# Sums of weight blocks for the second down stage: made by accumulating DMA instead of additions on Pool

## The chip, the cores and the metric

The kernel runs on one core of one Trainium2 chip. The metric is device time in microseconds (us) of one execution; lower is better. TensorE (PE) multiplies, VectorE (DVE), ScalarE (ACT) and Pool (GpSimd) work on tiles in SBUF, SyncE (SP) issues most loads. "HBM" and "DRAM" mean the same memory. DMA transfers of all queues run on the core's 16 DMA engines.

## The reference

One decoder layer on 512 tokens of width 1024: a SwiGLU feed-forward stage, a token-mixing stage of several attention branches, and a second feed-forward stage. What matters here is the frame and the feed-forward:

```python
def swiglu(x, w_gu, w_down):
    g, u = jnp.split(x @ w_gu, 2, axis=-1)
    return (jax.nn.silu(g) * u) @ w_down
...
        x = x + 0.5 * rms_norm(swiglu(rms_norm(x, ffn1_norm_pre[l]), ffn1_w_gu[l], ffn1_w_down[l]),
                               ffn1_norm_post[l])
        h = rms_norm(x, mix_norm_pre[l])
...
        x = x + rms_norm(merged @ w_out[l], mix_norm_post[l])
        x = x + 0.5 * rms_norm(swiglu(rms_norm(x, ffn2_norm_pre[l]), ffn2_w_gu[l], ffn2_w_down[l]),
                               ffn2_norm_post[l])
```

The inner width is D_FF = 2816, that is 22 blocks of 128 rows; all is float32. Each product is made of three products of rounded high and low parts.

## The kernel before

The stages follow one another: up products of the first feed-forward (to about 240 us), its down products (to 360 us, `down`, L2152), projections and attention (to 811 us), up products of the second feed-forward (to 1046 us), and its down products (`down_product`, L2178, and `down_rest`, L2197). Weights go through a ring of two slots: SP loads `ring_raw` (1 MB a slot in two DMAs), ACT copies it rounded into `ring_hi` (`hi`, L872), DVE subtracts into `ring_lo` (`lo`, L1327; in halves, L1338, before the projections), PE multiplies.

In the second down stage 16 of the 22 row blocks of the weight `w2_down` are not multiplied plainly but by a scheme of seven products in place of eight. For each of two groups g of 8 row blocks, the weight is cut into four blocks B11, B12, B21, B22 (4 x 128 rows by 512 columns each, 1 MB). Besides B11, B21 and B22 the scheme needs four sums T1 to T4 of blocks, and on DVE sums of the matching blocks of the activations (`sum_h`, from L1503), and on the finished products `close_21`, `close_22`, `close_12`. In the kernel before

T3 = B22 - B12, T1 = B12 - B11, T2 = T3 + B11 = B22 - B12 + B11, T4 = B21 - T2.

These eight sums (four for each g) don't depend on any input but the weight. Pool makes them ahead, in the first down stage, when the upper part of the activation memory is free, and stores them in DRAM as `down_weight_sums` (`sums_dram`). SP loads them into the ring in the second down stage (`load_down_block`, L607).

The order of Pool's program is written out by hand. After the first up stage (`rows_read(0)`) it loads a gain, issues the loads of the four blocks of g = 0 (`load_blocks(0)`, four buffers `down_block`, L744), builds a vector of position biases by 107 small copies (L773), stores it (L776), waits, and issues five DMAs that spread it over rows in DRAM (L784). Then come `sum_blocks(0)`, a wait for its four stores, `load_blocks(1)` into the same buffers, and `sum_blocks(1)`. Each `sum_blocks` is four additions (L751, L754, L757, L760), each followed by a store. After that stands `add_x(0)` (L729 to L735), and only then the wait for the last stores.

`add_x(0)` adds the normed result of the first feed-forward stage to x: six additions (L734) of 128x512, each after DVE has made `y_gained` (`add_y`, L1380). `y_gained` has room for two of the four token tiles, so DVE's work on tile 2 waits for Pool's first two additions, and on tile 3 for the first four. PE's `renew_x` waits for the first four additions before it transposes the new x (L2036), and the projection (L2012) waits for the transposed and scaled x. DVE reaches `add_y` only after it has split the first projection weights (L1338).

Of the kernel before, what the change touches and what calls it, by code (L numbers as in the profile page):

```python
# [29 lines left out]
ALU = mybir.AluOpType  # L30
# [3 lines left out]
P = 128  # L34
S, D, F = 512, 1024, 2816
# [146 lines left out]
def layer_kernel(nc, x, g1_pre, w1_gu, w1_down, g1_post, gm_pre, w_in, pos_k, cw1_k, cw2_k,  # L182
# [218 lines left out]
    blocks_loaded, sum_made, sums_stored = sem("blocks_loaded"), sem("sum_made"), sem("sums_stored")  # L401
# [175 lines left out]
    with block:  # L577
# [128 lines left out]
        def _(pool):  # L706
# [33 lines left out]
            def load_blocks(g):  # L740

                for block_sb, (k_half, c) in zip(blocks_sb, ((0, 0), (0, 1), (1, 1), (1, 0))):
                    k0 = 8 * g + 4 * k_half
                    pool.dma_start(block_sb[:, :, :], by_k(w2_down[k0 * P:(k0 + 4) * P, c * S:c * S + S])).then_inc(blocks_loaded, 16)  # L744

            def sum_blocks(g):

                b11, b12, b22, b21 = [b[:, :, :] for b in blocks_sb]
                t3, t1, t2, t4 = [sums_dram[g, i] for i in range(4)]
                pool.wait_ge(blocks_loaded, 64 * (g + 1))  # L750
                pool.tensor_tensor(b22, b22, b12, ALU.subtract).then_inc(sum_made, 1)  # L751
                pool.wait_ge(sum_made, 4 * g + 1)
                pool.dma_start(t3, b22).then_inc(sums_stored, 16)
                pool.tensor_tensor(b12, b12, b11, ALU.subtract).then_inc(sum_made, 1)  # L754
                pool.wait_ge(sum_made, 4 * g + 2)
                pool.dma_start(t1, b12).then_inc(sums_stored, 16)
                pool.tensor_tensor(b11, b22, b11, ALU.add).then_inc(sum_made, 1)  # L757
                pool.wait_ge(sum_made, 4 * g + 3)
                pool.dma_start(t2, b11).then_inc(sums_stored, 16)
                pool.tensor_tensor(b21, b21, b11, ALU.subtract).then_inc(sum_made, 1)  # L760
                pool.wait_ge(sum_made, 4 * g + 4)
                pool.dma_start(t4, b21).then_inc(sums_stored, 16)
# [3 lines left out]
            load_blocks(0)  # L766
# [8 lines left out]
            pool.wait_ge(vec_filled, 2)  # L775
            pool.dma_start(vec_dram, bias_vec[0:20, :]).then_inc(scratch_stored, 16)  # L776
# [8 lines left out]
            sum_blocks(0)  # L785
            pool.wait_ge(sums_stored, 64)
            load_blocks(1)
            pool.wait_ge(scratch_stored, 96)
            sum_blocks(1)

            add_x(0)
            pool.wait_ge(sums_stored, 128)
# [517 lines left out]
        def _(dve):  # L1310
# [85 lines left out]
            def ffn(base, f, p):  # L1396
# [107 lines left out]
                def sum_h(which, g):  # L1504
# [3 lines left out]
                    if which == 1:  # L1508
                        dve.wait_ge(w_used, first_down)
                        e = dve.tensor_tensor(h_sum[1, g][:, :, :], a21, a22, ALU.add)  # L1510
                    else:
                        dve.wait_ge(h_summed, H_SUMS.index((2 if which == 4 else 1, g)) + 1)
                    if which == 2:
                        e = dve.tensor_tensor(h_sum[2, g][:, :, :], h_sum[1, g][:, :, :], a11, ALU.subtract)
                    if which == 3:
                        e = dve.tensor_tensor(a21, a11, a21, ALU.subtract)
                    if which == 4:
                        e = dve.tensor_tensor(h_sum[4, g][:, :, :], a12, h_sum[2, g][:, :, :], ALU.subtract)
# [11 lines left out]
                def close_22(row):  # L1530

                    bank = ps[:, 5 + 2 * row, :]
                    dve.wait_ge(down_taken, 6 + row + 1)
                    dve.wait_ge(down_closed, 2 * row + 2)
                    dve.tensor_tensor(bank, bank, u3_sb[:, row, :], ALU.add).then_inc(down_closed, 1)

                def close_12(row):
# [4 lines left out]
                    dve.tensor_tensor(bank, bank, m5_sb[:, row, :], ALU.add).then_inc(down_closed, 1)  # L1542
# [1090 lines left out]
```

## Time and profile before

| what | us |
|---|---|
| median of 3 runs (1158.41 to 1161.01) | 1160.94 |
| profiled execution | 1163.08 |
| its span | 1161.4 |
| PE busy in the span | 1140.4 |
| DVE busy | 769.9 |
| ACT busy | 538.7 |
| Pool busy | 144.5 |
| share of the chain that ended last: PE | 91% |

The span runs from the first to the last instruction; the profiled execution's own time is 1.7 us longer. Busy time of an engine says how much it works, not what it holds up: that is read from waits (who was idle until whom) and from the chain that ended last. In the views below a row of a timeline is start, duration, engine, line, operation and tiles, and in brackets the idle time before it with its releaser.

### The profile page before, as it was taken

How to read it: one execution, taken by the hardware profiler on the slowest of the kernel's cores; microseconds unless marked ns; L12 is line 12 of the kernel's file. 1: busy time of each engine (PE TensorE's matmuls, PEld its weight loads, DVE VectorE, ACT ScalarE, POOL GpSimd, SP SyncE). 2: the span in 40 equal slices, each digit the busy share in tenths (PEclk: the TensorE clock that was granted, in tenths of full speed). 3: DMA queues.
4: the chain of work that ended last, by engine and by line, in shares of the span. 5: the costliest groups of instructions: out<-in, count | busy, mean ns of one | idle time of the engine just before them, and what ended most of it. 6: DMA issues, size and time to landing. Idle time of an engine off the chain costs nothing.

```text
span 1161.4 us, 18860 instructions
## 1 busy us (share of the span) xinstructions
PE 1140.4 (98%) x7172; PEld 998.5 (86%) x7172; DVE 769.9 (66%) x1181; ACT 538.7 (46%) x992; POOL 144.5 (12%) x222
## 2 busy tenths in 40 slices
PE   9999999999998999999989999999999999999998
PEld 7889999988886888887967888888789999998886
DVE  5888888846527336445888353663589888888763
ACT  6255555532214312246778322334535555556543
POOL 0000000078467010000014100002000000000002
PEclk9999999999999999999999999999999999999999
DMA  7323333387976352453200222323222333335541
GB/s 218 109 66 96 99 103 108 109 303 211 376 254 202 93 144 74 143 177 114 76 3 2 73 75 107 127 73 109 73 73 74 109 108 108 108 109 200 200 162 72
DMA packets 145150, 146.46 MB, mean 126 GB/s; under 512 B 4660, under 2 KB 125660, under 8 KB 144044
## 3 DMA queue, kind: packets, MB, share of 16 engines
q1 hardware_dynamic: 137568, 114.31, 32.2%
q0 software_dynamic: 7408, 31.27, 7.7%
q8 instruction: 41, 0.67, 0.3%
q14 instruction: 21, 0.17, 0.0%
q10 hardware_dynamic: 112, 0.03, 0.0%
HBM read 132.76 MB, written 17.29 MB: 129 GB/s over the span
## 4 chain that ended last, share of the span: by engine, by line
PE 91%; DVE 4%; ACT 2%; issue 1%; DMA 0%; POOL 0%; SPq 0%; DVEq 0%; ACTq 0%
PE ps L2012 29%; PE ps L2119 28%; PE ps L2152 8%; PE ps L2178 6%; PE ps L2307 4%; PE ps L2602 4%; PE ps L2197 3%; PE ps L2586 2%; DVE ring_lo L1327 1%; PE ps L2438 1%; PE ps L2460 1%; PE ps L2574 1%; PE ps L2379 1%; PE ps L2369 1%; PE ps L2390 1%
## 5 line engine op out<-in xcount | busy, mean ns | idle before, releaser
L1327 DVE TENSOR_TENSOR ring_lo<-ring_raw,ring_hi 128x2048 fp32r<-128x2048 f32 (+1 forms) x60 | 146.6, 2444 | 124.8 <-ACT ring_hi L872 124.8
L872 ACT ACTIVATE ring_hi<-ring_raw 128x2048 fp32r<-128x2048 f32 (+1 forms) x60 | 112.9, 1884 | 206.4 <-PE ps L2012 72.9
L2012 PE MATMUL ps<-xn_hi,ring_hi 128*128 128x512 f32 x480 | 190.4, 397 | 2.4 <-DVE xn_lo L1352 2.3
L2012 PE MATMUL ps<-xn_lo,ring_hi 128*128 128x512 f32 x480 | 188.1, 392 | 0.0
L2012 PE MATMUL ps<-xn_hi,ring_lo 128*128 128x512 f32 x480 | 188.0, 392 | 0.0
L2119 PE MATMUL ps<-s_hi,ring_hi 128*128 128x256 f32 x512 | 144.9, 283 | 0.0
L2119 PE MATMUL ps<-s_lo,ring_hi 128*128 128x256 f32 x512 | 144.9, 283 | 0.0
L2119 PE MATMUL ps<-s_hi,ring_lo 128*128 128x256 f32 x512 | 144.9, 283 | 0.0
L2012 PEld LDWEIGHTS ps<-xn_hi,ring_hi 128*128 128x128 f32 x480 | 90.8, 189 | 21.6 <-issue 3.5
L2119 PE MATMUL ps<-x_hi,ring_lo 128*128 128x256 f32 x384 | 108.7, 283 | 0.0
L2119 PE MATMUL ps<-x_lo,ring_hi 128*128 128x256 f32 x384 | 108.7, 283 | 0.0
L2119 PE MATMUL ps<-x_hi,ring_hi 128*128 128x256 f32 x384 | 108.7, 283 | 0.0
L2012 PEld LDWEIGHTS ps<-xn_hi,ring_lo 128*128 128x128 f32 x480 | 90.9, 189 | 19.2
L2012 PEld LDWEIGHTS ps<-xn_lo,ring_hi 128*128 128x128 f32 x480 | 90.8, 189 | 18.0
L2119 PEld LDWEIGHTS ps<-s_hi,ring_hi 128*128 128x128 f32 x512 | 98.3, 192 | 0.0
L2119 PEld LDWEIGHTS ps<-s_lo,ring_hi 128*128 128x128 f32 x512 | 98.3, 192 | 0.0
L2119 PEld LDWEIGHTS ps<-s_hi,ring_lo 128*128 128x128 f32 x512 | 98.3, 192 | 0.0
L958 ACT ACTIVATE ring_hi<-t_raw 128x512 fp32r<-128x512 f32 x122 | 76.0, 626 | 30.4 <-DVE t_raw L1471 19.2
L1456 DVE TENSOR_TENSOR ring_lo<-t_raw,ring_hi 128x512 fp32r<-128x512 f32 x122 | 83.2, 683 | 4.7 <-ACT ring_hi L958 4.7
L1456 DVE TENSOR_TENSOR ring_lo<-ring_raw,ring_hi 128x512 fp32r<-128x512 f32 x96 | 65.7, 686 | 30.1 <-ACT ring_hi L958 30.1
L958 ACT ACTIVATE ring_hi<-ring_raw 128x512 fp32r<-128x512 f32 x96 | 60.0, 627 | 32.8 <-DMA ring_raw<-in_ffn_w_gu 25.5
L2119 PEld LDWEIGHTS ps<-x_hi,ring_hi 128*128 128x128 f32 x384 | 73.7, 192 | 0.1
(339 smaller groups left out, 2359.3 us busy)
## 6 DMA issues: line engine op xcount, KB each, us to landing
ring_raw<-in_ffn_w_gu SPq DMA_DIRECT2D x86, 512.0 KB, 5.0
ring_raw<-in_w_in SPq DMA_DIRECT2D x42, 512.0 KB, 4.7
ring_raw<-in_ffn_w_down SPq DMA_DIRECT2D x40, 512.0 KB, 4.6
down_block<-in_ffn_w_down POOLq DMA_DIRECT2D x8, 1024.0 KB, 13.8
down_weight_sums<-down_block POOLq DMA_DIRECT2D x8, 1024.0 KB, 7.9
ring_raw<-down_weight_sums SPq DMA_DIRECT2D x16, 512.0 KB, 4.0
ring_raw<-in_w_out SPq DMA_DIRECT2D x8, 512.0 KB, 4.0
bias_rows_sparse<-bias_by_distance POOLq DMA_DIRECT2D x1, 2560.0 KB, 14.2
```

The source lines that it names most:

```text
L872: e = act.activation(dst, src, ACT.Copy)
L958: act.activation(by_tile(block_at(0, f, b)), weights_of(f, i, u, b), ACT.Copy).then_inc(blk_hi[b] if b < 6 else hi_ready, 1)
L1327: e = dve.tensor_tensor(dst, src, f32(r), ALU.subtract)
L1456: dve.tensor_tensor(by_tile(block_at(1, f, b)), weights_of(f, i, u, b), f32(by_tile(block_at(0, f, b))), ALU.subtract).then_inc(blk_lo[b] ...
L2012: e = pe.matmul(ps[:, 2 * (slot if pair is None else pair) + c, :], part(a, slot, k * 256 + c * P, P), xn[b][:, k, :], start=(k == 0 and i ...
L2119: e = pe.matmul(ps[:, bank, 0:256], block_at(a, f, b)[:, k * P:(k + 1) * P], (x_hi, x_lo)[x][b][:, k, :], start=(b in (B11, T1) and k == 0 ...
L2152: e = pe.matmul(ps[:, j, :], tokens[b], part(a, ring_slot(n0), kk * D + c * S, S), start=(n == 0 and kk == 0 and q == 0), stop=(n == DOWN ...
L2178: e = pe.matmul(ps[:, bank, :], tokens[b][:, k, row * P:row * P + P], part(a, ring_slot(n0), k * S, S), start=(m in (M1, M4, M5) and g == ...
L2197: e = pe.matmul(ps[:, j, :], tokens[b], part(a, ring_slot(n0), kk * D + c * S, S), start=False, stop=(n == 2 and kk == 1 and q == 2), skip ...
L2307: e = pe.matmul(ps[:, V_BANK[i // 2][t], :], xn[b][:, 4 * (i % 2) + kk, tokens], part(a, ring_slot(n), kk * S, S), start=(i % 2 == 0 and k ...
L2586: e = pe.matmul(ps[:, m % 4, :], part(a, ring_slot(n), k * S + (m % 4) * P, P), ynp[b][:, k, :], start=(k == 0 and q == 0), stop=(k == 3 a ...
L2602: e = pe.matmul(ps[:, 2 * t + c, :], xn[b][:, k, t * P:t * P + P], part(a, ring_slot(n), kk * D + c * S, S), start=(k == 0 and q == 0), st ...
```

## The change

The sums are chosen without a minus sign, so that each can be made by adding blocks onto one another: T1 = B11 + B12, T3 = B12 + B22, T2 = T1 + B22, T4 = T2 + B21. Pool adds nothing itself now: a block is loaded plainly into a buffer, the next is loaded onto it with `accum_op=ALU.add` (read from DRAM, added to what is in SBUF), and the result is stored. The four buffers hold T1 and T3 of both groups g at once. B12 and B22 of each g are read twice: there are 4 plain loads, 8 accumulating loads and 8 stores, of 1 MB each, where there were 8 plain loads, 8 additions and 8 stores. The wait for the last stores now stands before `add_x(0)`. In the second down stage the signs are turned on DVE: `sum_h` 1, 2 and 4, `close_22` and `close_12` compute the negative or the difference in one instruction.

```diff
--- before.py
+++ after.py
@@ -398,7 +398,7 @@
         sem("y_seeded"), sem("z_taken"), sem("t_taken"), sem("c22_taken"), sem("c12_taken"), sem("silu_ready"))
     x_joined, x_normed, x_mixed, sx_hi, sx_lo = sem("x_joined"), sem("x_normed"), sem("x_mixed"), sem("sx_hi"), sem("sx_lo")
     dve_chain = sem("dve_chain")
-    blocks_loaded, sum_made, sums_stored = sem("blocks_loaded"), sem("sum_made"), sem("sums_stored")
+    blocks_summed, sums_stored = sem("blocks_summed"), sem("sums_stored")
     h_summed, down_taken, down_closed = sem("h_summed"), sem("down_taken"), sem("down_closed")
 
     f32 = lambda ap: ap.bitcast(F32)
@@ -737,33 +737,35 @@
             def rows_read(f):
                 pool.wait_ge(w_used, (FFN1, FFN2)[f] + UP)
 
-            def load_blocks(g):
-
-                for block_sb, (k_half, c) in zip(blocks_sb, ((0, 0), (0, 1), (1, 1), (1, 0))):
-                    k0 = 8 * g + 4 * k_half
-                    pool.dma_start(block_sb[:, :, :], by_k(w2_down[k0 * P:(k0 + 4) * P, c * S:c * S + S])).then_inc(blocks_loaded, 16)
-
-            def sum_blocks(g):
-
-                b11, b12, b22, b21 = [b[:, :, :] for b in blocks_sb]
-                t3, t1, t2, t4 = [sums_dram[g, i] for i in range(4)]
-                pool.wait_ge(blocks_loaded, 64 * (g + 1))
-                pool.tensor_tensor(b22, b22, b12, ALU.subtract).then_inc(sum_made, 1)
-                pool.wait_ge(sum_made, 4 * g + 1)
-                pool.dma_start(t3, b22).then_inc(sums_stored, 16)
-                pool.tensor_tensor(b12, b12, b11, ALU.subtract).then_inc(sum_made, 1)
-                pool.wait_ge(sum_made, 4 * g + 2)
-                pool.dma_start(t1, b12).then_inc(sums_stored, 16)
-                pool.tensor_tensor(b11, b22, b11, ALU.add).then_inc(sum_made, 1)
-                pool.wait_ge(sum_made, 4 * g + 3)
-                pool.dma_start(t2, b11).then_inc(sums_stored, 16)
-                pool.tensor_tensor(b21, b21, b11, ALU.subtract).then_inc(sum_made, 1)
-                pool.wait_ge(sum_made, 4 * g + 4)
-                pool.dma_start(t4, b21).then_inc(sums_stored, 16)
+            def add_blocks(dst, k_half, c, w_down, g, first=False):
+
+                src = by_k(w_down[(8 * g + 4 * k_half) * P:(8 * g + 4 * k_half + 4) * P, c * S:c * S + S])
+                if first:
+                    pool.dma_start(dst, src).then_inc(blocks_summed, 16)
+                else:
+                    pool.dma_start(dst, src, accum_op=ALU.add).then_inc(blocks_summed, 16)
+
+            def store_sum(which, src, g):
+                pool.dma_start(sums_dram[g, DOWN_SUMS.index(which)], src).then_inc(sums_stored, 16)
+
+            summed, stored = [0], [0]
+
+            def wait_summed(n):
+
+                summed[0] += n
+                pool.wait_ge(blocks_summed, 16 * summed[0])
+
+            def wait_stored(n):
+
+                stored[0] += n
+                pool.wait_ge(sums_stored, 16 * stored[0])
 
             rows_read(0)
             load_gain(g1_post)
-            load_blocks(0)
+            both = [(g, blocks_sb[2 * g][:, :, :], blocks_sb[2 * g + 1][:, :, :]) for g in range(2)]
+            for g, a, b in both:
+                add_blocks(a, 0, 0, w2_down, g, first=True)
+                add_blocks(b, 0, 1, w2_down, g, first=True)
             pool.memset(bias_vec[0:20, :], MASKED).then_inc(vec_filled, 1)
             pool.wait_ge(small_loaded, 16)
             pool.tensor_scalar(neg_tab[0:20, :], tab[0:20, :], -1.0, None, ALU.mult).then_inc(tab_negated, 1)
@@ -773,6 +775,10 @@
                 e = pool.tensor_copy(bias_vec[0:20, first:first + step * (n - 1) + 1:step], neg_tab[0:20, b:b + 1].broadcast_to([20, n]))
             e.then_inc(vec_filled, 1)
             pool.wait_ge(vec_filled, 2)
+            wait_summed(4)
+            for g, a, b in both:
+                add_blocks(a, 0, 1, w2_down, g)
+                add_blocks(b, 1, 1, w2_down, g)
             pool.dma_start(vec_dram, bias_vec[0:20, :]).then_inc(scratch_stored, 16)
             pool.wait_ge(scratch_stored, 16)
 
@@ -782,14 +788,21 @@
                 src = bass.AP(tensor=vec_dram.tensor, offset=head * TAB_W + at0,
                               ap=[[0, rows], [TAB_W, heads], [1, width]])
                 pool.dma_start(dst, src).then_inc(scratch_stored, 16)
-            sum_blocks(0)
-            pool.wait_ge(sums_stored, 64)
-            load_blocks(1)
+            wait_summed(4)
+            for g, a, b in both:
+                store_sum(T1, a, g)
+                store_sum(T3, b, g)
+            wait_stored(4)
+            for which, k_half, c in ((T2, 1, 1), (T4, 1, 0)):
+                for g, a, b in both:
+                    add_blocks(a, k_half, c, w2_down, g)
+                wait_summed(2)
+                for g, a, b in both:
+                    store_sum(which, a, g)
+                wait_stored(2)
             pool.wait_ge(scratch_stored, 96)
-            sum_blocks(1)
 
             add_x(0)
-            pool.wait_ge(sums_stored, 128)
             pool.wait_ge(w_used, PROJ)
             pool.dma_start(wg_raw[:, :, :], by_k(w_in[:, GN:GN + 24])).then_inc(wg_loaded, 16)
             for dst, w2 in ((w2k[:, :, 0, :], cw2_k), (w2k[:, :, 1, :], cw2_k), (w2v[:, :, :], cw2_v)):
@@ -1507,15 +1520,17 @@
                     dve.wait_ge(h_ready, UP * f + 8 * g + 8)
                     if which == 1:
                         dve.wait_ge(w_used, first_down)
-                        e = dve.tensor_tensor(h_sum[1, g][:, :, :], a21, a22, ALU.add)
+                        e = dve.tensor_tensor(h_sum[1, g][:, :, :], a22, a21, ALU.subtract)
                     else:
                         dve.wait_ge(h_summed, H_SUMS.index((2 if which == 4 else 1, g)) + 1)
                     if which == 2:
-                        e = dve.tensor_tensor(h_sum[2, g][:, :, :], h_sum[1, g][:, :, :], a11, ALU.subtract)
+                        e = dve.scalar_tensor_tensor(out=h_sum[2, g][:, :, :], in0=h_sum[1, g][:, :, :], scalar=-1.0, in1=a11,
+                                                     op0=ALU.mult, op1=ALU.subtract)
                     if which == 3:
                         e = dve.tensor_tensor(a21, a11, a21, ALU.subtract)
                     if which == 4:
-                        e = dve.tensor_tensor(h_sum[4, g][:, :, :], a12, h_sum[2, g][:, :, :], ALU.subtract)
+                        e = dve.scalar_tensor_tensor(out=h_sum[4, g][:, :, :], in0=a12, scalar=-1.0, in1=h_sum[2, g][:, :, :],
+                                                     op0=ALU.mult, op1=ALU.subtract)
                     e.then_inc(h_summed, 1)
 
                 def close_21(row):
@@ -1532,14 +1547,16 @@
                     bank = ps[:, 5 + 2 * row, :]
                     dve.wait_ge(down_taken, 6 + row + 1)
                     dve.wait_ge(down_closed, 2 * row + 2)
-                    dve.tensor_tensor(bank, bank, u3_sb[:, row, :], ALU.add).then_inc(down_closed, 1)
+                    dve.scalar_tensor_tensor(out=bank, in0=bank, scalar=-1.0, in1=u3_sb[:, row, :], op0=ALU.mult,
+                                             op1=ALU.subtract).then_inc(down_closed, 1)
 
                 def close_12(row):
 
                     bank = ps[:, 1 + 2 * row, :]
                     dve.wait_ge(w_used, first_down + 12)
                     dve.wait_ge(down_taken, 6 + row + 1)
-                    dve.tensor_tensor(bank, bank, m5_sb[:, row, :], ALU.add).then_inc(down_closed, 1)
+                    dve.scalar_tensor_tensor(out=bank, in0=bank, scalar=-1.0, in1=m5_sb[:, row, :], op0=ALU.mult,
+                                             op1=ALU.subtract).then_inc(down_closed, 1)
 
                 def down_mixed():
 
```

On Pool, from the end of the bias vector's copies on, before the change (down_block_93 to 96 are the four buffers, in the order of `blocks_sb`):

```order
L776 DMA bias_by_distance<-bias_vec 20x2560 [waits vec_filled]
L784 DMA bias_rows_sparse<-bias_by_distance 1024x1x640 [waits scratch_stored]
L784 DMA bias_rows_dense<-bias_by_distance 512x1x384
L784 DMA bias_rows_strided<-bias_by_distance 512x1x256 x2
L784 DMA bias_rows_compressed<-bias_by_distance 256x1x1024
L751 TENSOR_TENSOR down_block_95<-down_block_95,down_block_94 128x2048 [waits blocks_loaded]
L753 DMA down_weight_sums<-down_block_95 128x2048 [waits sum_made]
L754 TENSOR_TENSOR down_block_94<-down_block_94,down_block_93 128x2048
```

The same place after the change:

```order
L746 DMA down_block_93<-in_ffn_w_down 128x4x512 [waits blocks_summed,vec_filled]
L746 DMA down_block_94<-in_ffn_w_down 128x4x512
L746 DMA down_block_95<-in_ffn_w_down 128x4x512
L746 DMA down_block_96<-in_ffn_w_down 128x4x512
L782 DMA bias_by_distance<-bias_vec 20x2560
L790 DMA bias_rows_sparse<-bias_by_distance 1024x1x640 [waits scratch_stored]
L790 DMA bias_rows_dense<-bias_by_distance 512x1x384
L790 DMA bias_rows_strided<-bias_by_distance 512x1x256 x2
L790 DMA bias_rows_compressed<-bias_by_distance 256x1x1024
L749 DMA down_weight_sums<-down_block_93 128x2048 [waits blocks_summed]
L749 DMA down_weight_sums<-down_block_94 128x2048
```

Four accumulating loads now stand ahead of the vector's store, and the additions behind the bias rows are gone.

On Pool ahead of `add_x(0)` (L734), before the change:

```order
L757 TENSOR_TENSOR down_block_93<-down_block_95,down_block_93 128x2048
L759 DMA down_weight_sums<-down_block_93 128x2048 [waits sum_made]
L760 TENSOR_TENSOR down_block_96<-down_block_96,down_block_93 128x2048
L762 DMA down_weight_sums<-down_block_96 128x2048 [waits sum_made]
L734 TENSOR_TENSOR x_tok<-y_gained,x_tok 128x512 [waits z_ready] x6
L794 DMA wg_raw<-in_w_in 128x8x24 [waits w_used,sums_stored]
```

The same place after the change:

```order
L746 DMA down_block_93<-in_ffn_w_down 128x4x512 [waits sums_stored]
L746 DMA down_block_95<-in_ffn_w_down 128x4x512
L749 DMA down_weight_sums<-down_block_93 128x2048 [waits blocks_summed]
L749 DMA down_weight_sums<-down_block_95 128x2048
L746 DMA down_block_93<-in_ffn_w_down 128x4x512 [waits sums_stored]
L746 DMA down_block_95<-in_ffn_w_down 128x4x512
L749 DMA down_weight_sums<-down_block_93 128x2048 [waits blocks_summed]
L749 DMA down_weight_sums<-down_block_95 128x2048
L734 TENSOR_TENSOR x_tok<-y_gained,x_tok 128x512 [waits z_ready,scratch_stored,sums_stored]
L734 TENSOR_TENSOR x_tok<-y_gained,x_tok 128x512 [waits z_ready] x5
```

The wait for the stores (`sums_stored`) has moved from behind the six additions of x to ahead of the first.

## Rows read from the trace of the kernel before

**Rows 1.** The page, busy time, share of the span and instructions of each engine.

```profile
PE 1140.4 (98%) x7172; PEld 998.5 (86%) x7172; DVE 769.9 (66%) x1181; ACT 538.7 (46%) x992; POOL 144.5 (12%) x222
```

**Rows 2.** Waits of PE, whole span: waiting <- for whom: us in total, times, longest.

```profile
PE ps L2152 <- DVE ring_lo L1327: 0.5, 1, 0.5
```

**Rows 3.** Chain of waits, 345 to 380 us (start, us, what), and PE's timeline.

```profile
352.05 2.95 issue
...
357.73 5.00 POOL x_tok L734 x4
...
367.50 2.12 PE ps L2012 x6
...
362.77 2.33 PE L2036 MATMUL ps<-ident,x_tok 128*128 128x128 f32 x16 [2.58 <-POOL x_tok L734]
```

**Rows 4.** Chain of waits at the mixing stage's end, 805 to 820 us.

```profile
804.87 6.14 PE ps L2602 x27
...
815.21 2.59 PE ps L2012 x6
```

**Rows 5.** Timeline of Pool in the first down stage.

```profile
267.89 0.60 POOL L776 DMA_DIRECT2D bias_by_distance<-bias_vec  x1 [0.29 <-POOL bias_vec L773]
271.93 0.88 POOL L784 DMA_DIRECT2D bias_rows_sparse<-bias_by_distance  x1 [3.44 <-DMA bias_by_distance<-bias_vec]
...
299.35 0.56 POOL L762 DMA_DIRECT2D down_weight_sums<-down_block  x1 [0.30 <-POOL down_block L760]
...
310.15 3.03 POOL L744 DMA_DIRECT2D down_block<-in_ffn_w_down  x4 [10.24 <-DMA down_weight_sums<-down_block]
...
354.27 0.56 POOL L762 DMA_DIRECT2D down_weight_sums<-down_block  x1 [0.30 <-POOL down_block L760]
```

**Rows 6.** Groups of Pool by line: busy us, mean ns, idle before (two of four).

```profile
L751 POOL TENSOR_TENSOR down_block<-down_block,down_block 128x2048 f32<-128x2048 f32 x2 | 11.2, 5613 | 17.0 <-DMA down_block<-in_ffn_w_down 17.0
L754 POOL TENSOR_TENSOR down_block<-down_block,down_block 128x2048 f32<-128x2048 f32 x2 | 10.4, 5195 | 0.0
```

**Rows 7.** Timeline of DVE in the first down stage.

```profile
263.54 2.29 DVE L1327 TENSOR_TENSOR ring_lo<-ring_raw,ring_hi 128x2048 fp32r<-128x2048 f32 x1 [7.44 <-ACT ring_hi L872]
...
274.42 7.97 DVE L1327 TENSOR_TENSOR ring_lo<-ring_raw,ring_hi 128x2048 fp32r<-128x2048 f32 x1 [7.45 <-ACT ring_hi L872]
...
350.50 5.70 DVE L1338 TENSOR_TENSOR ring_lo<-ring_raw,ring_hi 128x1024 fp32r<-128x1024 f32 x2 [6.49 <-ACT ring_hi L882]
```

**Rows 8.** Landing of `down_block`: round two's loads 1-2, then 3-4; store 299.35; stores 336-355.

```profile
DMA to landing us min/median/max: 7.9/9.7/11.5
...
DMA to landing us min/median/max: 13.5/15.6/17.6
...
DMA to landing us min/median/max: 10.5/10.5/10.5
...
DMA to landing us min/median/max: 4.2/4.6/5.3
```

**Rows 9.** Pool's queue: packets, MB, share of 16 engines; 320 to 325, 271.9 to 309.9 us.

```profile
q0 software_dynamic: 496, 1.90, 100.0%
...
q0 software_dynamic: 1856, 9.70, 72.8%
```

**Rows 10.** Busy us (x count) of PE, PEld, DVE, ACT, POOL; granted clock, DMA share, GB/s.

```profile
368.00:370.00 2.00, 2.00 (x8) 1.51 (x7) 1.33 (x3) 2.00 (x3) 2.00 (x4) 0.60 0.41 82
```

**Rows 11.** DVE: second down stage's timeline; two groups by line (busy us, mean ns).

```profile
1057.47 1.22 DVE L1514 TENSOR_TENSOR h_sum<-h_sum,hT 128x1024 f32<-128x1024 f32 x1
1059.79 2.29 DVE L1327 TENSOR_TENSOR ring_lo<-ring_raw,ring_hi 128x2048 fp32r<-128x2048 f32 x1 [1.09 <-ACT ring_hi L872]
...
L1456 DVE TENSOR_TENSOR ring_lo<-t_raw,ring_hi 128x512 fp32r<-128x512 f32 x122 | 83.2, 683 | 4.7 <-ACT ring_hi L958 4.7
L1352 DVE SCALAR_TENSOR_TENSOR xn_lo<-ps,gains,xn_hi 128x512 fp32r<-128x512 f32 x24 | 17.3, 747 | 11.2 <-ACT xn_hi L903 11.0
```

**Rows 12.** Issue to landing of SP's ring loads (L591), 240 to 362 us.

```profile
DMA to landing us min/median/max: 3.7/7.1/11.0
```

## The prediction

> **What bounds the kernel now.** I read four views in this order. The page's busy times come first: TensorE (PE) is busy for 98% of the span [rows 1], so the time can only fall where PE waits, and it rises with every new wait of PE. Second, PE's own waits: only two of them touch this change, 2.6 us for Pool's residual addition (L734, `add_x`) and 0.5 us for a ring slot split by VectorE (DVE) [rows 2, 3]. Third, the chain of waits at the end of the first down stage [rows 3]: the reader is to see that PE's last product of the stage ends at 362.77 - 2.58 = 360.19 us, and that the next projection starts at 367.50, 7.3 us later. Between them stand a DVE split of the next ring slot that is held up for 2.95 us, and then Pool's first four additions of `add_x(0)` from 357.73 to 362.73. At the end of the mixing stage the same code has PE's last product end at 804.87 + 6.14 = 811.01 and the next one start at 815.21, 4.2 us later [rows 4]; there Pool is on time and DVE is not held up. Fourth, Pool's own timeline [rows 5]: it is free at 267.9 us, makes the sums of the second down matrix in two rounds, issues its last store at 354.27 and then meets `add_x(0)` on time. So Pool has about 357.7 - 354.8 = 3 us to spare in this stage. This is the margin on which all hangs.
>
> **What the change removes.** Eight additions on Pool go, 5.2 to 5.6 us each, 42 us in sum [rows 6]. They lie off PE's path, yet they cost DVE time. A split of one ring slot (128x2048) takes 2.29 us with Pool idle and 7.97 us beside Pool's addition, and the last two splits of the stage take 5.70 us together, with the 2.95 us gap of [rows 3] in them [rows 7]. The first of these is PE's 0.5 us wait. The second delays the first `y_gained` of the stage's end. Without Pool's additions both go: at most 0.5 us, plus 7.3 - 4.2 = 3.1 us if `add_x(0)` also starts early. The full gain is 3.6 us, and 3.1 of it need Pool's sums to be finished before about 354.7, three microseconds earlier than `add_x(0)` starts now.
>
> **What it adds.** The sums are now made by transfers: 4 plain loads, 8 accumulating loads and 8 stores of 1 MB each, against 8 loads and 8 stores. They stand in a chain: four loads; four accumulates; four stores; then twice two accumulates and two stores, each behind a wait for the one before. Behind the last store wait stands `add_x(0)` on Pool; before, the wait for the last stores came after it. The store of the bias vector, too, is now queued behind four accumulates on Pool's one DMA queue, and the spreading of the bias rows waits for it.
>
> **The chain, priced first as if an accumulate cost a plain load.** The loads of the start land by about 262 us as before, under the bias copies, and cost nothing. The first accumulate is issued where the vector's store is now, at 267.9.
> - Four accumulates: four loads in a row took from the issue at 310.15 to landing 17.6 us after the last issue at 312.4, so 19.9 us [rows 5, 8]: 287.8.
> - Bias vector behind them: about 2 us of its landing, an estimate from the gap 267.89 to 271.93 [rows 5], half of which lies under the accumulates: 289.8.
> - Bias rows, then four stores: the same 9.7 MB went from 271.93 to 299.35 + 10.5 = 309.85, 37.9 us, with Pool's queue at 72.8% of the DMA engines [rows 5, 8, 9], so it was set by the transfers and not by Pool's pace: 327.7.
> - Two accumulates: the first two loads of the second round took 310.15 to 310.9 + 11.5, 12.3 us [rows 5, 8]. Two stores: one alone took 4.2 to 5.3 us [rows 8], and one block has all the DMA engines for 5 x 1.05 / 1.90 = 2.76 us [rows 9], so two take about 7.5. Twice 12.3 + 7.5 = 39.6: 367.3.
>
> The low end takes a block at 2.76 / 0.728 = 3.8 us beside the ring's loads and 1.4 us (4.2 - 2.76) for the fixed part: 16.6 for four, 9.0 for two, 6.9 for two stores, and gives 267.9 + 16.6 + 2 + 37.9 + 2 x 15.9 = 356.2. So even at a load's price the chain ends between 356.2 and 367.3, middle 361.8, against a need at 357.73: 1.5 us early to 9.6 us late.
>
> **The price of an accumulate.** No row of the kernel before has one. Below, it can't cost less than the plain load of the same block, since it moves the same bytes from HBM to SBUF. Above, it reads HBM, reads the block in SBUF and writes it back: the traffic of a load and of a store, so two transfers of a block, 3.8 us more each beside the ring's loads. Eight of them are 8 x 3.8 = 30.4 us, all in the chain. I take this end, because the second read is a real transfer through the same 16 engines, which were already full: 386.6 to 397.7, middle 392.2, 34.4 us after 357.73. Both ends stay in the range.
>
> The Trainium skill speaks against this change here: "Collectives: The Full Stack", in "The bandwidth ceiling: the fold count and why AG ≠ RS ≠ AR", says that adding in a transfer is slower not by the addition but by two source reads on one ring, with a measured ratio of 1.93. By that rule the eight accumulates would add 0.93 x 30.4 = 28.3 us to the chain and the time would be about 1193; at one read it would be about 1165. No row here shows which.
>
> **What waits.** Behind Pool's late `add_x(0)` stand DVE's `y_gained` of the last two token tiles (its two buffers must be taken), then PE's transposes, then the whole projection. Nothing later gives the time back, since PE is the bound there. So PE waits 34.4 us more. TensorE's granted clock fell to 0.60 of full speed, so towards the lower of its two levels, at 368 to 370 us, after the present pause of PE [rows 10]. That is already paid once; a longer pause may stretch it. I put 0 to 2 us on that, in the range.
>
> **Parts at nothing.** In the second down stage four sums of 128x1024 and four bank closings of 128x512 change from TENSOR_TENSOR to SCALAR_TENSOR_TENSOR, to turn signs. The form with two ALU steps took 747 ns for 128x512 where the other took 683 [rows 11], 9% more and perhaps less with a constant in it, so 0.1 us on each sum of 1.22. DVE idles 1.09 us behind such a sum [rows 11], so this is hidden. If that cover were gone it would be 4 x 0.11 + 4 x 0.06 = 0.7 us. Pool's issues cost 0.56 to 0.88 us each, as now [rows 5]. The moved bias rows are read only after the projection.
>
> **The sum.** The profiled execution took 1163.1 us with a span of 1161.4; + 34.4 for the chain, - 0.5 for DVE: 1197.0. The median of the runs is 1160.9, 2.2 below it, so the forecast is 1160.9 + 33.9 = **1195 us**.
>
> **Rivals.**
> - *An accumulate costs about a load.* For it: the adding itself may be free, and the DMA engines were full only part of the stage. Against it: the second read. Chain end 356.2 to 367.3, middle 4.1 us late; less 0.5 for DVE: 1164.5, range 1159 to 1170.
> - *The sums are early and DVE is free (faster).* One mechanism: with no addition on Pool, the splits at 350.5 end near 353, `y_gained` and `add_x(0)` start 3 us sooner, and the pause of 7.3 us shrinks to 4.2. It decides at 354.7: the chain must end before. That needs 1.5 us less than my lowest price. Time 1160.9 - 3.6 = 1157.3.
> - *Accumulates dearer than two transfers, or the ring starved.* The ring's loads land in 3.7 to 11.0 us with 7.1 as median [rows 12], against a step of PE of about 10.9 us (360.19 - 240 over 11 steps of `down`). If accumulates held the engines for three transfers each, the chain would be 4.1 + 60.8 = 65 us late, 1225, and the ring would come short besides.
> - That the change does not do what it says can be ruled out: the rows of Pool's order show eight accumulates and no addition on blocks.
>
> **Chances.** Accumulate at about two transfers (chain 13 to 55 us late): 0.56. At about a load: 0.28, of which 0.10 lie within 3.5 us of now. Early and faster: 0.06. Dearer than 55 us: 0.10. A measurement of this kernel can tell 0.3%, 3.5 us, from no change. So faster 0.06, same 0.10, slower 0.84. The range of 8 in 10 leaves out the early cases and the far end: 1163 to 1218.
>
> **What would show it.** Right: in Pool's timeline the first `add_x` at 390 us or so instead of 357.7, released by a DMA of `down_weight_sums`; PE's wait for L734 grown from 2.6 to near 37 us, and no 7.97 us split on DVE any more. The time from an accumulate's issue to landing tells its price: about 35 us for the last of four if two transfers, about 18 if one. Wrong: Pool waiting for `y_gained` at `add_x(0)`, as it does now; or PE waiting for DVE in the second down stage; or ScalarE waiting for ring loads between 270 and 340.

## The result and the profile after

The changed kernel takes 1188.7 us as median (4 runs, 1188.0 to 1190.4) against 1160.2 us before: a ratio of 1.025 with a 95% interval of 1.0232 to 1.0268, 28.5 us slower. The forecast was 1195 with a range of 1163 to 1218.

The page of the changed kernel, busy time by engine and then the chain that ended last by engine:

```profile
PE 1138.3 (96%) x7172; PEld 998.3 (84%) x7172; DVE 746.1 (63%) x1181; ACT 539.0 (45%) x992; POOL 110.0 (9%) x218
...
PE 82%; DMA 9%; POOL 4%; DVE 2%; issue 1%; ACT 1%; SPq 0%; DVEq 0%; ACTq 0%
```

Pool and DVE do less than in [rows 1], and the time rose. Transfers are 9% of the chain that ended last; before they were 0%. Where, Pool's timeline of the changed kernel tells (start, duration, what, and in brackets the idle time before it with its releaser):

```profile
267.86 5.30 POOL L746 DMA_DIRECT2D down_block<-in_ffn_w_down  x4 [0.31 <-POOL bias_vec L775]
...
298.89 0.88 POOL L790 DMA_DIRECT2D bias_rows_sparse<-bias_by_distance  x1 [25.19 <-DMA bias_by_distance<-bias_vec]
...
338.17 2.66 POOL L746 DMA_DIRECT2D down_block<-in_ffn_w_down  x2 [33.45 <-DMA down_weight_sums<-down_block]
354.45 1.14 POOL L749 DMA_DIRECT2D down_weight_sums<-down_block  x2 [13.63 <-DMA down_block<-in_ffn_w_down]
364.81 2.63 POOL L746 DMA_DIRECT2D down_block<-in_ffn_w_down  x2 [9.22 <-DMA down_weight_sums<-down_block]
378.63 1.14 POOL L749 DMA_DIRECT2D down_weight_sums<-down_block  x2 [11.19 <-DMA down_block<-in_ffn_w_down]
385.42 7.37 POOL L734 TENSOR_TENSOR x_tok<-y_gained,x_tok 128x512 f32<-128x512 f32 x6 [5.65 <-DMA down_weight_sums<-down_block]
```

These are the steps of the chain as the prediction laid it out, and each ends in Pool waiting for a transfer. The residual additions start at 385.42 instead of 357.73 [rows 3], released by a store of the sums. In PE's timeline of the changed kernel the wait of 2.58 us [rows 3] has become:

```profile
390.40 4.53 PE L2053 MATMUL ps<-ident,x_tok 128*128 128x128 f32 x20 [31.05 <-POOL x_tok L734]
...
395.94 0.47 PE L2029 MATMUL ps<-xn_hi,ring_hi 128*128 128x512 f32 x1 [1.02 <-DVE xn_lo L1365]
```

PE's last down product ends at 390.40 - 31.05 = 359.35 and the projection starts at 395.94: a pause of 36.6 us against 7.3. It is 29.3 us longer and begins 0.8 us earlier, so the projection starts 28.4 us later (395.94 - 367.50), about as much as the medians differ. The agreement to a tenth is luck: the spans of the two profiled executions differ by 24.9 us (1186.3 against 1161.4), because the one of the kernel before, at 1163.1 us slower than its median, lost about 1.6 us to a lower granted clock behind each of two pauses of PE (the last section shows them), and the one of the changed kernel did not.

DVE's split of a ring slot at 274 us, which took 7.97 us beside Pool's additions [rows 7], is normal in the changed kernel:

```profile
274.35 2.29 DVE L1340 TENSOR_TENSOR ring_lo<-ring_raw,ring_hi 128x2048 fp32r<-128x2048 f32 x1 [7.43 <-ACT ring_hi L885]
```

**The price of an accumulate** can now be read. These are rows of Pool's DMA queue (packets, MB, share of 16 engines) in the changed kernel, first from 267.9 to 297.9 us (four accumulates and the bias vector's store), then from 364.8 to 378.6 us (two accumulates with no other load beside them) and from 368 to 375 us (the middle of the same two), then from 378.6 to 385.4 us (two stores):

```profile
q0 software_dynamic: 2156, 4.40, 80.1%
...
q0 software_dynamic: 1056, 2.10, 86.2%
...
q0 software_dynamic: 709, 1.42, 112.1%
...
q0 software_dynamic: 288, 2.10, 75.3%
```

And the four plain loads of the kernel before, 310.1 to 330 us:

```profile
q0 software_dynamic: 1088, 4.19, 59.3%
```

An accumulated block of 1 MB is 1056 / 2 = 528 packets, a plain load of one 1088 / 4 = 272. It held the 16 engines for 0.862 x 13.8 / 2 = 5.95 us (and 0.801 x 30.0 / 4 = 6.0 in the full stretch), a plain load for 0.593 x 19.9 / 4 = 2.95, a store for 0.753 x 6.8 / 2 = 2.6. An accumulate is two transfers: the ratio to a load is 2.02. These are sums of the packets' times, which can overlap (the 112.1% in the middle stretch). By the pace there, 1.42 MB in 7.0 us, a block of 1.05 MB passes in 5.2 us, against 2.76 for a plain load alone [rows 9]: a ratio of 1.87. The Trainium skill's rule of two source reads, which it states for a collective operation between cores ("Collectives: The Full Stack", in "The bandwidth ceiling: the fold count and why AG ≠ RS ≠ AR", ratio 1.93), agrees with these two numbers. That it is the second read and not the adding which takes the time is not shown here; the doubled packets speak for it.

### The profile page after: what moved, and what is told of

Its sections match the earlier page's. It is cut to its first block, busy times and chain, and to the rows that moved or that the text cites. A ratio compares the mean times of both kernels' runs of the same rounds, so it can differ in the third digit from the quotient of the medians.

```text
span 1186.3 us, 18856 instructions
## 1 busy us (share of the span) xinstructions
PE 1138.3 (96%) x7172; PEld 998.3 (84%) x7172; DVE 746.1 (63%) x1181; ACT 539.0 (45%) x992; POOL 110.0 (9%) x218
## 4 chain that ended last, share of the span: by engine, by line
PE 82%; DMA 9%; POOL 4%; DVE 2%; issue 1%; ACT 1%; SPq 0%; DVEq 0%; ACTq 0%
PE ps L2029 28%; PE ps L2136 27%; PE ps L2195 6%; DMA down_weight_sums<-down_block 4%; PE ps L2324 4%; PE ps L2619 4%; PE ps L2214 3%; DMA down_block<-in_ffn_w_down 2%; DMA bias_by_distance<-bias_vec 2%; PE ps L2603 2%; POOL bias_vec L775 2%; PE ps L2455 1%; PE ps L2477 1%; PE ps L2591 1%; PE ps L2053 1%
## 5 line engine op out<-in xcount | busy, mean ns | idle before, releaser
L1340 DVE TENSOR_TENSOR ring_lo<-ring_raw,ring_hi 128x2048 fp32r<-128x2048 f32 (+1 forms) x60 | 135.3, 2256 | 142.6 <-ACT ring_hi L885 142.6
```

What stands on the lines that cost most here:

```text
L1340: e = dve.tensor_tensor(dst, src, f32(r), ALU.subtract)
```

## The experiments

All kernels ran beside runs of the kernel before. Its median was 1160.3 us beside the first four experiments (plain loads, the wait behind the additions, the additions between the steps, and the kernel before without additions of blocks) and 1161.3 us beside the other four.

### The chain with plain loads

```diff
-                    pool.dma_start(dst, src, accum_op=ALU.add).then_inc(blocks_summed, 16)
+                    pool.dma_start(dst, src).then_inc(blocks_summed, 16)
```

> The changed kernel with its eight accumulating loads as plain loads of the same blocks; the chain of waits is the same, the sums are left out. If the accumulate's price is what makes the chain late (an accumulate held the DMA engines 5.95 us in the quiet stretch 364.8 to 378.6, a plain load 2.95), the chain's three accumulate steps of 29.9, 16.3 and 13.8 us shrink to about 19.9, 10.7 and 7.9, the first residual addition moves from 385.4 to about 364, and the time is about 1167 us. Rival: the chain of waits itself and the late start are what costs, and an accumulate is nearly free: 1183 to 1189 us.

Measured: 1165.9 us (ratio to before 1.0053, 1.0038 to 1.0069), 22.9 us less than the changed kernel. Its Pool timeline:

```profile
268.04 3.07 POOL L746 DMA_DIRECT2D down_block<-in_ffn_w_down  x4 [0.30 <-POOL bias_vec L775]
...
283.72 0.88 POOL L790 DMA_DIRECT2D bias_rows_sparse<-bias_by_distance  x1 [12.08 <-DMA bias_by_distance<-bias_vec]
...
323.67 1.54 POOL L746 DMA_DIRECT2D down_block<-in_ffn_w_down  x2 [34.13 <-DMA down_weight_sums<-down_block]
332.56 1.11 POOL L749 DMA_DIRECT2D down_weight_sums<-down_block  x2 [7.35 <-DMA down_block<-in_ffn_w_down]
342.81 1.53 POOL L746 DMA_DIRECT2D down_block<-in_ffn_w_down  x2 [9.14 <-DMA down_weight_sums<-down_block]
354.98 1.10 POOL L749 DMA_DIRECT2D down_weight_sums<-down_block  x2 [10.65 <-DMA down_block<-in_ffn_w_down]
363.26 7.38 POOL L734 TENSOR_TENSOR x_tok<-y_gained,x_tok 128x512 f32<-128x512 f32 x6 [7.17 <-DMA down_weight_sums<-down_block]
```

So the accumulates' extra price is 385.42 - 363.26 = 22.2 us of the lateness, and the chain's own length at a load's price the other 5.5 (363.26 - 357.73). The expectation had this sum right (364) by misses that cancelled: its three steps of 19.9, 10.7 and 7.9 us took 15.7, 8.9 and 12.2. Step by step against the changed kernel: the first four accumulates and the vector 31.0 against 15.7 us, 3.8 more for each accumulate; the next two 16.3 against 8.9, 3.7 each; the last two 13.8 against 12.2, only 0.8 each. The last step differs in what ran beside it. These are SP's loads (q1) of the ring, in this experiment from 342.8 to 354.9 us, while the same step of the changed kernel had none:

```profile
q1 hardware_dynamic: 2430, 1.41, 45.4%
```

The ring's loads took 0.454 x 12.1 = 5.5 us of the engines there, and the two loads themselves 5.6. In the changed kernel the ring was full by then, since PE stood still.

### The last wait behind the additions

```diff
-                wait_stored(2)
-            pool.wait_ge(scratch_stored, 96)
-
-            add_x(0)
+                if which == T2:
+                    wait_stored(2)
+            pool.wait_ge(scratch_stored, 96)
+
+            add_x(0)
+            wait_stored(2)
```

> The changed kernel with the wait for the last two stores moved from ahead of the six residual additions to behind them, all else the same. Theory (Pool's additions wait for the end of the whole chain, and only that): they start right behind the issue of the last stores, at about 379.8 instead of 385.4, and the time is 5.6 us lower, 1183 us. Rival: PE waits for something else too (the two token tiles' buffers, the clock), and gets back less than 3 us.

Measured: 1183.1 us, 5.6 less than the changed kernel, as expected; that it fits to the tenth is luck, since the four runs lie between 1181.9 and 1185.1. In the trace Pool's additions start at 380.25, 5.2 us sooner, and the projection at 390.78, 5.2 us sooner too: PE gets back what Pool gets back, one for one, and the rival (less than 3 us) falls.

### The additions between the chain's steps

```diff
                 for g, a, b in both:
                     store_sum(which, a, g)
+                if which == T2:
+                    add_x(0)
                 wait_stored(2)
             pool.wait_ge(scratch_stored, 96)
-
-            add_x(0)
```

> The changed kernel with the six residual additions on Pool moved up: behind the issue of the second pair of stores (354.5 to 355.6 us in the trace of the changed kernel), ahead of the wait for them and of the last two accumulates. Theory: the transfers themselves hold up nobody but Pool, so nearly all of the 28.5 us comes back, and with no additions of blocks on Pool the splits on DVE are not held up, so the pause of PE shrinks from 7.3 towards 4.2 us: 1157 to 1158 us, 0.3% below the kernel before. Rival: the doubled traffic costs PE or the ring elsewhere: 1162 us or more.

Measured: 1158.6 us (11 runs), ratio 0.9986 (0.9974 to 0.9997), just above the expected 1157 to 1158 and well below the rival's 1162. 30 of the changed kernel's microseconds are gone with all eight accumulates in place, so the transfers themselves don't hold up PE; the place of the additions on Pool does. PE and Pool in this kernel:

```profile
355.34 7.48 POOL L734 TENSOR_TENSOR x_tok<-y_gained,x_tok 128x512 f32<-128x512 f32 x6
...
360.43 0.77 PE L2054 MATMUL ps<-ident,x_tok 128*128 128x128 f32 x5 [1.15 <-POOL x_tok L734]
...
365.15 0.47 PE L2030 MATMUL ps<-xn_hi,ring_hi 128*128 128x512 f32 x1 [1.15 <-DVE xn_lo L1366]
```

PE's pause is 5.9 us (359.28 to 365.15), not yet 4.2: Pool issued two stores until 355.3, and the first `y_gained` was ready at about 353.4.

### One step earlier

```diff
                 for g, a, b in both:
                     add_blocks(a, k_half, c, w2_down, g)
+                if which == T2:
+                    add_x(0)
                 wait_summed(2)
```

(and the `add_x(0)` behind the chain is gone, as in the run before)

> As the run with the six residual additions between the chain's steps, but one step earlier: behind the issue of the second set of accumulates (338 to 341 us), ahead of the wait for them. Pool is then idle when the first y_gained is ready (353.5 us) and no longer issues stores until 355.3. Theory (the pause of PE ends with Pool's fourth addition until that is early enough, then at 4.2 us): the pause is 4.2 us as in the run without additions, against 5.9, so 1.7 us less than that run: about 1157 us. Rival: PE's pause is already set by the last token tile there, and nothing changes: 1158.6 us.

Measured: 1156.6 us (6 runs), ratio 0.9953 (0.9936 to 0.9969). The start of its chain of waits at the stage's end, and the projection's:

```profile
344.88 15.21 PE ps L2170 x67
360.09 0.02 issue
360.11 0.04 ACT squares L939
...
364.30 1.62 PE ps L2030 x6
```

The pause is 4.2 us, the same as at the mixing stage's end [rows 4]: Pool is no longer in the chain. How much of the time the 1.7 us of pause are can't be told from these runs: in the two traces the projection starts only 0.85 us sooner (364.30 against 365.15), since PE's last product ended 0.8 us later here, and the ratios differ by 0.33%, 3.8 us, with intervals nearly as wide. This version makes all the sums and leaves nothing out; it is faster than both kernels, by 4.7 us of 1161.3. It uses the change's transfers and puts Pool's residual additions where they are due. Its chain of transfers ends later than the changed kernel's, the last two stores being issued at 387.5 instead of 378.6 us, and that costs nothing.

### The kernel before without Pool's additions of blocks

```diff
-                pool.tensor_tensor(b22, b22, b12, ALU.subtract).then_inc(sum_made, 1)
-                pool.wait_ge(sum_made, 4 * g + 1)
                 pool.dma_start(t3, b22).then_inc(sums_stored, 16)
-                pool.tensor_tensor(b12, b12, b11, ALU.subtract).then_inc(sum_made, 1)
-                pool.wait_ge(sum_made, 4 * g + 2)
                 pool.dma_start(t1, b12).then_inc(sums_stored, 16)
...
```

> The kernel before with Pool's eight additions left out; the blocks are loaded and stored as they are, so the sums are wrong. It measures what these additions cost through DVE. Theory: the 0.5 us wait of PE and 3.1 of its 7.3 us pause go, 3.6 us: 1156.6 us against 1160.2. Rival: only the 0.5 us goes and the pause is set by something else: 1159.7 us.

Measured: 1155.1 us (6 runs), ratio 0.9963 (0.995 to 0.9976), 5.2 us by the medians and 4.3 by the ratio. The interval, 2.8 to 5.8 us, holds the 3.6 of the theory and not the rival's 0.5. Its chain of waits at the stage's end:

```profile
359.27 0.02 issue
359.29 0.04 ACT squares L917
...
363.48 1.62 PE ps L2004 x6
```

The pause is 4.2 us, as the theory has it (7.3 - 3.1), and it begins 0.9 us sooner (not all of it by the additions: in the run before this one, which has none on Pool either, it began at 360.09). What the theory left out is the clock in and behind the pause. These are stretches with busy time by engine, granted clock, DMA share and GB/s; first this kernel, then the kernel before, whose stretch from 368 to 370 us stands in [rows 10]:

```profile
364.00:366.00 2.00, 2.00 (x11) 1.64 (x10) 1.30 (x2) 2.00 (x3) 2.00 (x4) 1.00 0.56 96
366.00:368.00 2.00, 2.00 (x12) 1.60 (x11) 1.78 (x2) 1.46 (x3) 2.00 (x5) 1.00 0.77 287
...
370.00:372.00 2.00, 2.00 (x7) 1.57 (x6) 1.77 (x2) 0.78 (x2) 2.00 (x5) 0.54 0.88 313
```

After its 7.3 us pause the kernel before ran for about 3.5 us at the lower clock, which cost 1.6 us (7.8 us from the projection's start to the end of its first 24 products, against 6.2 here). That is one execution. In the trace of the next experiment ("signs alone"), which has the same additions and the same wait of 2.58 us for Pool, the lower clock came earlier, on the transposes, and the first 24 products took 6.2 us:

```profile
364.00:366.00 2.00, 2.00 (x12) 2.00 (x11) 1.97 (x4) 0.00 (x0) 2.00 (x3) 0.50 0.00 0
```

There it cost 0.5 us: from Pool's fourth addition to the projection's start 5.3 us passed (363.09 to 368.40), against 4.8 in the kernel before (362.73 to 367.50). So by the traces the additions of blocks cost 4.1 to 5.2 us through DVE: 0.5 in the middle of the stage, 3.1 in the pause, and 0.5 to 1.6 by the clock.

### The second down stage's signs alone

```diff
-                        e = dve.tensor_tensor(h_sum[2, g][:, :, :], h_sum[1, g][:, :, :], a11, ALU.subtract)
+                        e = dve.scalar_tensor_tensor(out=h_sum[2, g][:, :, :], in0=h_sum[1, g][:, :, :], scalar=-1.0, in1=a11,
+                                                     op0=ALU.mult, op1=ALU.subtract)
...
-                    dve.tensor_tensor(bank, bank, m5_sb[:, row, :], ALU.add).then_inc(down_closed, 1)
+                    dve.scalar_tensor_tensor(out=bank, in0=bank, scalar=-1.0, in1=m5_sb[:, row, :], op0=ALU.mult,
+                                             op1=ALU.subtract).then_inc(down_closed, 1)
```

> The kernel before with only the second down stage's DVE instructions of the change (four sums and four bank closings in the two-step form, the first sum as a difference); Pool's sums keep their signs, so the result is wrong. Theory: each instruction takes what it took (1.22 us in the trace of the changed kernel) and nothing moves: 1160.3 us, within 0.1%. Rival: the two-step form costs DVE time that reaches PE, 0.7 us or more.

Measured: 1161.2 us, ratio 1.0001 (0.9989 to 1.0013): no change, as the theory has it. In its DVE timeline the two-step sum takes as long as the plain one of [rows 11]:

```profile
1054.60 1.22 DVE L1514 SCALAR_TENSOR_TENSOR h_sum<-h_sum,hT 128x1024 f32<-128x1024 f32 x1
```

### The bias vector's store ahead of the accumulates

```diff
+            pool.dma_start(vec_dram, bias_vec[0:20, :]).then_inc(scratch_stored, 16)
             wait_summed(4)
             for g, a, b in both:
                 add_blocks(a, 0, 1, w2_down, g)
                 add_blocks(b, 1, 1, w2_down, g)
-            pool.dma_start(vec_dram, bias_vec[0:20, :]).then_inc(scratch_stored, 16)
```

> The changed kernel with the store of the bias vector ahead of the four accumulates instead of behind them. Pool then waits under 1 us for the vector instead of 25.2 us. Theory (the chain is set by the transfers, which are the same): the first four sums' stores land at most 1 to 3 us sooner, 1186 to 1188 us. Rival (the wait of 25.2 us behind the accumulates is what delays the chain): 15 us or more less, 1165 to 1174 us.

Measured: 1182.3 us (ratio 1.0179, 1.0157 to 1.0201), 6.5 us below the changed kernel: neither what the theory said (1 to 3) nor the rival's 15. Its Pool timeline:

```profile
300.69 2.14 POOL L749 DMA_DIRECT2D down_weight_sums<-down_block  x4 [23.38 <-DMA down_block<-in_ffn_w_down]
333.85 2.66 POOL L746 DMA_DIRECT2D down_block<-in_ffn_w_down  x2 [31.01 <-DMA down_weight_sums<-down_block]
...
378.14 7.38 POOL L734 TENSOR_TENSOR x_tok<-y_gained,x_tok 128x512 f32<-128x512 f32 x6 [5.64 <-DMA down_weight_sums<-down_block]
```

The first stores' step ends at 333.85 instead of 338.17, 4.3 us sooner. The wait of 25.19 us was mostly the accumulates' own time, so the rival falls. Part of what is gained is a gap in the changed kernel between 297.3 and 301 us, in which the DMA engines stood idle or part idle while Pool waited for the vector's landing and issued the rows. Its stretch from 298 to 299 us (busy by engine, granted clock, DMA share, GB/s) and the next two:

```profile
298.00:299.00 1.00, 1.00 (x6) 0.84 (x5) 1.00 (x2) 0.00 (x0) 0.10 (x1) 1.00 0.00 0
299.00:300.00 1.00, 1.00 (x6) 0.83 (x5) 0.54 (x1) 0.00 (x0) 1.00 (x2) 1.00 0.63 90
300.00:301.00 1.00, 1.00 (x6) 0.82 (x5) 0.00 (x0) 0.00 (x0) 1.00 (x3) 1.00 0.68 233
```

By the shares these three, and the end of the one before (0.31), make 1.0 + 0.4 + 0.3 + 0.7 = 2.4 us. The next two steps gave 3.1 more, 14.8 and 8.7 us against 16.3 and 10.4, of 7.3 in all at the first addition (378.14 against 385.42). How they fall against the ring's loads may be the cause of the rest; that was not tried apart.

### The kernel before with its wait moved ahead

```diff
-            add_x(0)
             pool.wait_ge(sums_stored, 128)
+            add_x(0)
```

> The kernel before with its wait for the last stores moved from behind the six residual additions to ahead of them, as the change does. The last store is issued at 354.3 and lands 4.5 us later, at 358.8, against 357.7 where the additions start: theory 1 us more, 1161 us. Rival: the place of the wait alone costs several us, 1164 us or more.

Measured: 1162.7 us, ratio 1.0008 (0.9994 to 1.0022). Its chain of waits shows the store now in it, 1.3 us past the old start of 357.73:

```profile
354.46 4.51 DMA down_weight_sums<-down_block
358.97 0.07 issue
359.05 6.20 POOL x_tok L734 x5
```

The interval holds both 1 us and nothing. The place of the wait alone costs at most 2.6 us (0.22%); it hurts where the chain behind it is late.

## Why the prediction was right, point by point

**The bound, the margin and the mechanism** held: the chain of transfers outlived the time at which `add_x(0)` was due, PE paused, and no later stage gave it back. Of the signs laid down, the first addition came at 385.4 (390 or so), released by a store of the sums, PE's wait for it was 31.05 us (near 37), and the split of 7.97 us was gone. Moving the additions by 5.2 us moved the projection by 5.2, and moving them out of the chain brought all of the time back.

**An accumulate at two transfers** held: 5.95 us of the engines against 2.95. As 3.8 us of the chain for each, it held for six of eight (3.8 and 3.7). For the last two it was 0.8. The sign that I had laid down for it, 35 us from issue to landing for the last of four if two transfers and 18 if one, would have decided nothing alone: it took 27.6 us, half way between, and the plain load in its place 12.4. Both of my numbers were too high for the reason that follows.

**The size of the sum** was 34.4 us late and the chain was 27.7 us late, so the forecast of 1195 was 6.3 us too high, inside its range. What was mis-sized is mostly the price of the plain loads and not the 3.8 us added to it. Four loads and the vector behind them were priced at 18.6 to 21.9 us and took 15.7 with plain loads; the next two were priced at 9.0 to 12.3 and took 8.9. The high prices came from one stretch of the kernel before, 310.1 to 330 us, in which the queues kept the DMA engines busy for only 87% (59.3% by Pool's queue and 27.2% by the ring's). For the last pair the 3.8 us themselves failed. It was priced at 16.6 to 19.9 us and took 13.8: with plain loads it stood beside the ring's loads and took 12.2, but in the changed kernel the late chain had itself emptied the queue beside it (the ring was full and SP silent). The stores of the first pair went the other way, 10.4 us against 6.9 to 7.5, with the projection's first ring loads beside them. My low row gave 386.6 for the end at two transfers against 385.4 measured, and that is partly luck: its steps were 2.8 us too long twice, and 3.5 and 1.4 us too short. So the price of a transfer depends on what is in flight at its hour, and a chain that is late moves into other company.

**The rival at a load's price**, 1164.5 us with the chain's end at 361.8, was tried directly: 1165.9 and 363.3.

**The rival that ends faster** did not come in the changed kernel, since the chain ended long after 354.7. As a mechanism it held: with Pool free in time, the pause is 4.2 us and the time 1155 to 1157. I had sized it at 3.6 us; the run without additions gives 4.3 (2.8 to 5.8), and the traces 4.1 to 5.2 with the clock.

**The clock** had 0 to 2 us in the range, as a loss. It was small and had two signs. In the changed kernel the transposes ran at the lower of the two clocks, and the projection's products behind them at full clock:

```profile
392.00:394.00 2.00, 2.00 (x11) 2.00 (x10) 2.00 (x3) 0.00 (x0) 2.00 (x3) 0.50 0.00 0
...
396.00:398.00 2.00, 2.00 (x10) 1.64 (x11) 1.77 (x3) 2.00 (x4) 2.00 (x3) 1.00 0.48 90
```

The transposes and what hangs on them took 0.8 us more (390.35 to 395.94, against 362.73 to 367.50), the first 24 products 1.6 less. The 1.6 is no gain of the change: it is what this one execution of the kernel before lost, and the trace of "signs alone" did not lose it.

**The starving ring** did not come: no wait of ScalarE for a ring load is in the trace of the changed kernel between 240 and 400 us. **The parts at nothing** were nothing: the two-step sums took 1.22 us like the plain ones, not 0.1 more, and PE's wait for DVE in the second down stage is 0.6 us in both kernels.

## What to carry to other kernels

An accumulating DMA takes work from an engine and gives it to the transfers twice over (5.95 us of the DMA engines for a block here, against 2.95 for a plain load); before using it, count its blocks as two, and lay the whole chain of dependent transfers beside the time at which the issuing engine is next needed. If the chain is longer, look for another order before a shorter chain: put the engine's due work between two steps of it, ahead of the wait, as soon as its input is ready. Here that alone turned 2.5% slower into 0.5% faster.

## What the runs showed of the hardware that I had not expected

The spread between runs of one kernel follows the granted clock. In the kernel without additions of blocks the six runs took 1154.2, 1154.2, 1154.9 and 1155.2 us at a mean clock of 0.999 to 1.0, and 1156.8 and 1158.0 at 0.997 and 0.996. The profiled execution of the kernel before (clock 0.995, 1163.1 us) had the lower clock behind both of its pauses. Behind the mixing stage's pause, which no edit touched and which was 4.2 us in all ten traces, the products ran at the lower clock in some and at full clock in others: 0.51 from 817 to 819 us in the kernel before, 1.00 at the same place (808 to 810 us) in the kernel without additions.

```profile
817.00:819.00 2.00, 2.00 (x7) 1.51 (x7) 1.19 (x2) 1.51 (x2) 0.00 (x0) 0.51 0.00 0
...
808.00:810.00 2.00, 2.00 (x10) 1.65 (x11) 1.76 (x3) 2.00 (x3) 0.00 (x0) 1.00 0.00 0
```

The first 24 products behind it took 7.8 us in two traces (the kernel before, and the additions between the chain's steps) and 6.2 in the other eight. Behind the first down stage the clock stayed full through the three pauses of 4.2, 4.2 and 5.9 us. In the seven of 7.3 us and more it fell each time, and cost 1.6 us where it met the first products (the kernel before, and its wait moved ahead) and 0.5 to 0.8 us where it met the transposes (the other five). So a pause of PE costs its length and, in some executions, up to about 1.6 us more, and one profile doesn't tell which.
